# A hybrid decoder trunk on one core: weights in quarters, eight token transfers on two queues, and the first unit copied ahead of the last squares

## The reference, cut to what matters

```python
def rmsnorm(x, g):
    x32 = x.astype(jnp.float32)
    y = x32 * lax.rsqrt(jnp.mean(x32 * x32, axis=-1, keepdims=True) + EPS)
    return (y * g.astype(jnp.float32)).astype(x.dtype)
...
def token_mixers(a, W, i, C0, n0, m0, S0):
    z = a @ W['w_in'][i]
    mq, mk, mv, mi, mf, mo, gq, gk, gv, glr, gg, ga, gb = jnp.split(z, SPLIT_IDX, axis=-1)
...
def trunk(x, p, C0, n0, m0, S0, cv0, W):
    h = x
    for i in range(DEPTH):
        a = rmsnorm(h, W['norm_mix_g'][i])
        mix, C, n, m, Sf = token_mixers(a, W, i, C0[i], n0[i], m0[i], S0[i])
        h = h + mix
        f, cv = conv_ffn(rmsnorm(h, W['norm_ffn_g'][i]), W, i, cv0[i])
        h = h + f
        e = rmsnorm(h, W['norm_ple_g'][i])
        h = h + jax.nn.sigmoid(e @ W['w_ple_gate'][i]) * (p[i] @ W['w_ple_proj'][i])
    y = rmsnorm(h, W['final_norm_g'])
```

## Time and profile before

| | us |
|---|---|
| median of 3 runs | 1178.58 (1177.72 to 1179.01) |
| the profiled execution's own time | 1177.82 |
| its span | 1176.0 |
| PE busy in the span | 1166.6 |
| DVE busy | 756.6 |
| ACT busy | 393.9 |

### The profile page before, as it was taken

How to read it: one execution, slowest core, us unless ns; L and a number is a source line. 1 busy time by engine, 2 the same in 40 slices (tenths; PEclk the granted TensorE clock), 3 DMA queues, 4 the chain that set the end, 5 groups by cost and what they waited for, 6 DMA issues and landing times.

```text
span 1176.0 us, 21858 instructions
## 1 busy us (share of the span) xinstructions
PE 1166.6 (99%) x9191; PEld 1110.7 (94%) x9191; DVE 756.6 (64%) x1394; ACT 393.9 (33%) x579; POOL 4.4 (0%) x9
## 2 busy tenths in 40 slices
PE   9999999999999999999999999999999999999997
PEld 8999999999999999999999999999999999999997
DVE  6855568675777655664665667777777764233677
ACT  6243332133444322333333223333333322111545
POOL 0000000000000000000000000000000000000001
PEclk9999999999999999999999999999999999999999
DMA  6342232422313366554443542122122134223232
GB/s 221 109 150 84 97 108 91 145 73 93 113 68 109 113 223 238 179 171 142 151 143 130 174 155 72 72 76 104 72 75 105 62 102 147 94 75 114 72 108 82
DMA packets 48962, 138.56 MB, mean 118 GB/s; under 512 B 5460, under 2 KB 25108, under 8 KB 39776
## 3 DMA queue, kind: packets, MB, share of 16 engines
q1 hardware_dynamic: 16680, 89.65, 22.0%
q10 hardware_dynamic: 32184, 47.51, 12.0%
HBM read 113.15 MB, written 23.81 MB: 116 GB/s over the span
## 4 chain that ended last, share of the span: by engine, by line
PE 95%; DVE 2%; issue 1%; DMA 1%; ACT 1%; POOL 0%; ACTq 0%; POOLq 0%; DVEq 0%
PE ps L808 34%; PE ps L836 10%; PE ps L834 6%; PE ps L837 6%; PE ps L835 6%; PE ps L937 6%; PE ps L814 6%; PE ps L838 5%; PE ps L943 3%; PE ps L855 2%; PE aux L1100 1%; DMA xT<-in_xT 1%; PE aux L1164 1%; PE aux L995 1%; PE aux L1060 1%
## 5 line engine op out<-in xcount | busy, mean ns | idle before, releaser
L808 PE MATMUL ps<-apair,whi 128*128 128x288 f32 x1728 | 275.1, 298 | 0.7 <-ACT mq L2120 0.6
L808 PEld LDWEIGHTS ps<-apair,whi 128*128 128x128 f32 x1728 | 243.3, 189 | 4.9 <-issue 2.1
L1215 DVE TENSOR_TENSOR wlo<-wraw,whi 128x2048 fp32r<-128x2048 f32 (+1 forms) x82 | 176.1, 2147 | 74.8 <-ACT whi L1965 70.5
L1965 ACT ACTIVATE whi<-wraw 128x2048 fp32r<-128x2048 f32 (+1 forms) x87 | 156.4, 1797 | 107.1 <-PE ps L838 52.5
L836 PE MATMUL ps<-apair,whi 128*128 128x512 f32 x336 | 132.1, 393 | 0.0
L834 PE MATMUL ps<-apair,whi 128*128 128x320 f32 x336 | 105.0, 313 | 0.0
L837 PE MATMUL ps<-apair,wlo 128*128 128x320 f32 x336 | 104.2, 310 | 0.0
L835 PE MATMUL ps<-apair,whi 128*128 128x320 f32 x336 | 103.8, 309 | 0.0
L808 PE MATMUL ps<-apair,wlo 128*128 128x288 f32 x448 | 95.9, 296 | 0.0
L838 PE MATMUL ps<-apair,wlo 128*128 128x256 f32 x336 | 95.1, 283 | 0.0
L838 PEld LDWEIGHTS ps<-apair,wlo 128*128 128x128 f32 x336 | 63.2, 188 | 14.2
(11 more groups left out here) (419 smaller groups left out, 2094.0 us busy)
## 6 DMA issues: line engine op xcount, KB each, us to landing
wraw<-in_w_in SPq DMA_DIRECT2D x31, 1024.0 KB, 5.0
wraw<-in_w_up SPq DMA_DIRECT2D x21, 1024.0 KB, 4.9
gate_scratch<-stg ACTq DMA_DIRECT2D x32, 288.0 KB, 2.8
gt<-gate_scratch ACTq DMA_DIRECT2D x32, 288.0 KB, 2.9
wraw<-in_w_pgate SPq DMA_DIRECT2D x6, 1024.0 KB, 4.7
wraw<-in_w_down SPq DMA_DIRECT2D x8, 704.0 KB, 4.1
wraw<-in_w_down SPq DMA_DIRECT2D x8, 640.0 KB, 3.9
out_C_s<-st ACTq DMA_DIRECT2D x16, 256.0 KB, 3.0
```

Of the source, the lines that this page charges most:

```text
L808: mm = nc.tensor.matmul(ps[:, t % 2, a, 0:HALF], w, x(k)[:, a * HALF:(a + 1) * HALF], start=f, stop=e)
L1215: V.tensor_tensor(wlo[:, s, 0:n], wraw[:, s, 0:n], f32(whi[:, s, 0:n]), ALU.subtract)\
L1965: A.activation(whi[:, s, 0:n], wraw[:, s, 0:n], ACT.Copy).then_inc(split_hi, 1)
```

## The change: what it does

The two halves of unit 0's weights become a quarter, a quarter and a half. The tokens come in eight pieces of one block each. SP issues quarter 0, quarter 1, block 3, the second half, blocks 5 and 7 and the misc weights; ACT issues block 0, the gains, blocks 1 and 2 and, behind its first activation, blocks 4 and 6. DVE, not ACT, copies the high part of quarter 0. PE takes in each block all products of `ahi` before those of `alo`, with a wait for each. ACT copies the two tiles of unit 0 out before the last two squares. `rsum` moves from block 1 to block 3 of unit 1's first tile, `rspread` from block 6 of it to the start of the second tile, and DVE's low part of unit 1 stands ahead of `rsum`.

```diff
-    sched += [("misc",), ("rsum", 0), ("lo", 1), ("rspread", 0), ("misc_scale",)]
+    sched += [("misc",), ("lo", 1), ("rsum", 0), ("rspread", 0), ("misc_scale",)]
...
-MID = {("mq", 1, 0): {1: ("rsum", 0), 6: ("rspread", 0)},
+MID = {("mq", 1, 0): {3: ("rsum", 0)}, ("mq", 1, 1): {0: ("rspread", 0)},
...
-X_PIECES = [(0, 1), (1, 2), (2, 4), (4, 6), (6, 8)]
+X_PIECES = [(k, k + 1) for k in range(KT)]
...
-            sp.dma_start(gains[:, :, :], ins["gains"]).then_inc(gains_in, 16)
...
                 if u == 1:
-                    sp.wait_ge(x_in[3], 16)
+                    sp.wait_ge(x_in[5], 16)
...
                 if u == 0:
-                    sp.dma_start(wraw[:, 0, 0:UW // 2], ins["w_in"][0, :, 0:UW // 2]).then_inc(raw_first, 16)
+                    sp.dma_start(wraw[:, 0, quarter(0)], ins["w_in"][0, :, quarter(0)]).then_inc(raw_first[0], 16)
+                    sp.dma_start(wraw[:, 0, quarter(1)], ins["w_in"][0, :, quarter(1)]).then_inc(raw_first[1], 16)
+                    sp.dma_start(xT[:, 3:4, :], ins["xT"][:, 3:4, :]).then_inc(x_in[3], 16)
                     sp.dma_start(wraw[:, 0, UW // 2:], ins["w_in"][0, :, UW // 2:]).then_inc(raw_in[0], 16)
+                    for k in (5, 7):
+                        sp.dma_start(xT[:, k:k + 1, :], ins["xT"][:, k:k + 1, :]).then_inc(x_in[k], 16)
...
                     if k == 0:
                         pe.wait_ge(hi_first, 1)
+                    elif k == 2:
+                        pe.wait_ge(hi_second, 1)
...
-                    pe.wait_ge(a_hi, k + 1)
-                    pe.wait_ge(a_lo, k + 1)
-                    for n in range(2):
-                        col = (2 * k + n) * P
-                        for x in (ahi, alo):
+                    for x, ready in ((ahi, a_hi), (alo, a_lo)):
+                        pe.wait_ge(ready, k + 1)
+                        for n in range(2):
+                            col = (2 * k + n) * P
...
-                    if k == 0:
-                        pe.wait_ge(lo_first, 1)
+                    if k in (0, 2):
+                        pe.wait_ge(lo_first, k // 2 + 1)
...
                 if s[0] == "norm_in":
+                    dve.wait_ge(raw_first[0], 16)
+                    V.tensor_copy(whi[:, 0, quarter(0)], wraw[:, 0, quarter(0)]).then_inc(hi_first, 1)
                     dve.wait_ge(gains_in, 16)
...
-                        if k == 0:
-                            dve.wait_ge(hi_first, 1)
-                            V.tensor_tensor(wlo[:, 0, 0:UW // 2], wraw[:, 0, 0:UW // 2], f32(whi[:, 0, 0:UW // 2]),
+                        if k < 2:
+                            dve.wait_ge((hi_first, hi_second)[k], 1)
+                            V.tensor_tensor(wlo[:, 0, quarter(k)], wraw[:, 0, quarter(k)], f32(whi[:, 0, quarter(k)]),
...
-            for n, (k0, k1) in enumerate(X_PIECES):
-                act.dma_start(xT[:, k0:k1, :], ins["xT"][:, k0:k1, :]).then_inc(x_in[n], 16)
+            act.dma_start(xT[:, 0:1, :], ins["xT"][:, 0:1, :]).then_inc(x_in[0], 16)
+            act.dma_start(gains[:, :, :], ins["gains"]).then_inc(gains_in, 16)
+            for k in (1, 2):
+                act.dma_start(xT[:, k:k + 1, :], ins["xT"][:, k:k + 1, :]).then_inc(x_in[k], 16)
             act.wait_ge(init_done, 1)
             A.activation(stat[:, 0, :], stat[:, 1, :], ACT.Sqrt).then_inc(act_warm, 1)
+            for k in (4, 6):
+                act.dma_start(xT[:, k:k + 1, :], ins["xT"][:, k:k + 1, :]).then_inc(x_in[k], 16)
...
-                            if k == 0:
-                                act.wait_ge(raw_first, 16)
-                                A.activation(whi[:, 0, 0:UW // 2], wraw[:, 0, 0:UW // 2], ACT.Copy).then_inc(hi_first, 1)
+                            if k == 1:
+                                act.wait_ge(raw_first[1], 16)
+                                A.activation(whi[:, 0, quarter(1)], wraw[:, 0, quarter(1)], ACT.Copy).then_inc(hi_second, 1)
...
                     for k in range(KT):
+                        if k == KT - 2:
+                            for n in range(2):
+                                act.wait_ge(tile_ready, n + 1)
+                                A.activation(two(mq[:, n, :]), tile(n), ACT.Copy).then_inc(tile_free[n], 1)
                         if k >= 2:
                             act.wait_ge(in_sq_used, k - 1)
                         A.activation(sq[:, k % 2, :], xT[:, k, :], ACT.Square).then_inc(in_sq, 1)
```

More of the change, by code:

```diff
@@ L438, in build @@
         raw_in = sems("raw_in", 2)
-        raw_first = sem("raw_first")
+        raw_first = sems("raw_first", 2)
         hi_first = sem("hi_first")
+        hi_second = sem("hi_second")
         lo_first = sem("lo_first")
@@ L591, in both_of, with quarter @@
             return x[:, k - k0, :]
+        def quarter(q):
+            return slice(q * UW // 4, (q + 1) * UW // 4)
         def half_of(e):
@@ L2117, in _ @@
                         act.sem_inc(v_ready, 1)
-                    elif s[1] == 0:
-                        act.wait_ge(tile_ready, tt + 1)
-                        A.activation(two(mq[:, i, :]), tile(tt), ACT.Copy).then_inc(tile_free[tt], 1)
                     elif kind in ("mo", "gg", "ga", "gb"):
```

## The result

| | before | with the change |
|---|---|---|
| median, us | 1178.22 (1177.68 to 1179.01, 22 runs) | 1180.28 (1179.77 to 1181.38, 22 runs) |
| ratio | | 1.0018, 95% interval 1.0012 to 1.0023 |
| the profiled execution, us | 1177.82 | 1179.79 |
| its span, us | 1176.0 | 1178.0 |

I had forecast 1177.7, from a median of 1178.58 of the kernel before that 22 runs put at 1178.22. The time lies above my range, and the change is slower by somewhat more than run-to-run scatter, though by less than 0.2%. The two profiled executions differ by as much as the medians, so the traces can be compared directly. In these two executions the clock plays no part: the page's row reads as before, and the mean granted clock is 0.999 in both.

A forecast was written before the change was run, and what follows sets the result against it. PE was taken as the bound, busy 1166.6 of 1176.0 us. 1.15 (start) + 0.55 (blocks) + 0.55 (`mq`) - 0.5 (`rsum`) - 0.85 (three waits on DVE's chain) = 0.9 us gained: median 1177.7, range 1176.2 to 1179.5.

The forecast's parts named there:

- The bound, and what a gain must pass: Whole kernel: PE is the bound; the opening can give 2.2 us, then PE runs into DVE's chain three times.
- unit 3's low part: DVE's low part ended at 54.99, PE wanted it at 56.58: slack 1.59, gain at most 1.1 us.
- The wait for `mq`: PE before unit 1: the 0.55 us wait goes, since ACT's first copy is done at 21.2, before 21.8.
- First unit, start: PE's first unit starts at 6.75 instead of 7.90 and ends at 19.65 instead of 21.37: 1.7 us gained.
- What follows from the landing: ACT's copy of the second half begins at about 10.2 instead of 11.20, so D = 15.4; no stall on PE.
- The landing itself, 10.2: Second half of unit 0's weights lands at 10.2, taken between estimates of 8.8 and 11.8; before, 9.64.
- D: Time DVE is through with block 7's low part in the opening: forecast 15.4 (bounds 14.4 and 17.0), before 16.42.
- The spread: After `rsum` at 23.95, `rspread` starts at 29.85 and DVE reads it at 30.9; before, 30.37.
- S: How much later DVE's chain runs from its read of the spread on: D - 14.9, not under 0; forecast 0.5 us.
- the wait only changes its place: Rival: D about 16.2, wait at `rsum` and S both 1.3, gain at L1108 0.1, time 1178.5; chance 0.15.
- The slack at the `la` products: Last L1108 pair starts at 70.33, its bank free at 68.96: slack 1.37, gain at most 0.9 us, lasting to the end.
- late-fetch rival: Half lands at 11.8 or later, D 17.0 or more, PE stalls 1 us at block 4, S 2.1, time 1179.3; chance 0.15.

The follow-up runs named there:

- Experiment 8: Kernel before with only the gains moved, from first on SP to behind block 0 on ACT: 1180.39 against 1177.94 us, ratio 1.0017.
- experiment 1: Changed kernel with the load of the gains back at the head of SP's queue: 1180.47 us against 1177.92 for the kernel before, ratio 1.0020.
- 10: Changed kernel without its three token transfers on SP, all eight token blocks on ACT: 1180.19 us against 1178.10 for the kernel before, ratio 1.0019.
- 11: Kernel before with quarters behind the gains on SP, DVE copying quarter 0, reordered passes, one copy ahead, three memsets on GpSimd: 1178.03 against 1177.84 us.
- 9: Kernel before with tokens in eight one-block pieces, all on ACT, and unit 1 released behind block 5: 1177.73 against 1177.84 us, ratio 1.0002.
- 2: Kernel before with the change's order of ACT's copies, `rsum`, `rspread` and unit 1's low part, none of its transfers: 1179.28 against 1177.92 us.
- 4: Changed kernel with three of DVE's opening memsets moved to GpSimd, so DVE's stream is as long as before: 1179.94 us, ratio 1.0016.
- 5: Kernel before with one DVE memset cut into four, three entries more in its stream: 1178.52 against 1178.10 us, ratio 1.0006.
- 3: Changed kernel with the order of before (`sched`, `MID`, copies to `mq`), so the transfers alone: 1179.96 us against 1177.92 for the kernel before, ratio 1.0018.

## Why the prediction was wrong

**The bound, and what a gain must pass: right.** PE is the bound, and the waits of the opening came where the prediction put them, but for one: at `rsum` (forecast 0.5, measured 0.50), at unit 2 and at the `la` products. None was added at unit 3's low part: it came 2.15 late against a slack of 1.59, and PE was already 0.69 late there. The wait for `mq` went (0.55 forecast, 0.63 measured).

**First unit, start: wrong by 1.27 us.** "The gains, now behind block 0 on ACT, are covered in the same way, with about 0.7 us to spare." They land at 7.0, not under 6, and the first product is at 8.02. I took block 0 to land no later than the 4.5 us of the earlier trace rows, although it now stood opposite weights and not the gains; it took 5.2. Experiment 8 shows the place of the gains alone to be enough. It isn't what the 2 us are made of, though: in experiment 1 the start was mended and the time stayed.

**What follows from the landing: the step that failed most.** The landing itself, 10.2, came true. But I let ACT's copy begin at the landing, and dropped what stands ahead of it on ACT: blocks 1 and 2, which I had not given landings of their own. They came at 8.7 and 10.6, the copy at 11.97, and D was 17.18 instead of 15.4. From that copy to D it took 5.2 us, as forecast. What sets D, in the kernels that take the fetch apart:

| | tokens on both queues | tokens on ACT |
|---|---|---|
| gains behind block 0 on ACT | 17.18 (the change) | 17.16 (10), 16.95 (8, halves) |
| gains first on SP | 17.03 (1) | 16.64 (11), 16.20 (9, halves), 16.42 (before) |

Either half of the change's fetch alone holds D at 17. With the gains behind block 0 it is ACT's own queue that is late (in 8 the second half lands at 7.5 and in 10 at 9.1, and its copy begins at 11.4 and 11.9). With the gains first it is the second half (11.8 in 1). Only without both does D come down, with quarters by 0.4 alone, since the half still lands at 11.4 (11), with halves to the 16.4 of before or a little under. No kernel here came near 15.4. What delays the half behind two quarters in 11, where no tokens stand on SP, no run takes apart.

That the landing came true is luck. It was a choice between 8.8 and 11.8, and the 11.8 rests on a wrong reading: the 2.66 MB of before didn't move at 424 GB/s in 6.3 us but at a mean of 276 GB/s in 9.64. The lower bound of 14.4 for D has no working either; a landing at 8.8 would give 14.0.

**The spread: the form was right, the price too small.** My S = D - 14.9 gives 2.3 for D = 17.18, and 2.54 was measured. In all five kernels with the change's order (the change, 1, 2, 4, 10) the scale reaches DVE 15.7 to 15.8 us after D, where my sum has 15.5. I took S to be free until D = 14.9 and believed D to be near it. At the D of the kernel before it is 1.5 by the formula and 1.92 measured: the order loses by itself (0.9 us of waits in experiment 2), and I never worked that case out. The rival "the wait only changes its place" had it at 16.2 and priced it at +0.1 gain.

**The slack at the `la` products: 0.81, not 1.37.** I spaced four pairs that ran side by side by the pitch of products in a row.

**Two stops of DVE: not foreseen.** They cost 0.29 (a step of 0.35, of which 0.06 had come back before it) and 0.36, and moved with the number of entries that DVE has had before (experiments 4 and 5).

The sum: at the `la` products I had 1.37 - 0.5 = 0.87 gained, and it is 0.81 - 2.14 = 1.33 lost, which is 2.2 apart: 1.64 for the delay of DVE's chain (2.14, since the stop at `both`, 0.4, was gone) and 0.56 for the slack. The two stops are 0.65. Together 2.85, and 0.9 forecast gain to 2.0 measured loss is 2.9. The late-fetch rival (D at 17.0 or more, S 2.1, 1179.3) had the mechanism nearly whole. Its place of decision was wrong: it wanted a landing at 11.1, and D came by way of ACT's own queue. Its stall at block 4 didn't come, since PE itself had started 1.27 late. I gave it 0.15.

## What to carry to other kernels

A landing time isn't the time at which work on it starts: list everything that stands ahead on the engine, with a landing for each, and take the latest. Two queues that share the DMA engines are one race: what stands opposite a transfer counts as much as what stands ahead of it, and a tiny transfer that gates the first instruction belongs at the head of a queue, though what stands behind it may then land later (in experiment 1 the second half, at 11.8 instead of 10.2). A step that comes earlier on the bound engine is worth only as much as the next chain can follow, so work out that chain at the old timing too, before believing that a new order is free.

## What the hardware showed that I had not expected

- DVE stops for about half a microsecond, 0.35 to 0.4 of it beyond its usual gap, with nothing to wait for, before records 63, 191, 319 and 1599 of its stream as the trace counts them (one less than a multiple of 64 each, counted from 0), in the kernel before and in all kernels here whose stream is as long as its. In the change, 1, 3, 5 and 10, whose streams are three longer, it stops before 1087 and 1855 (17 and 29 times 64, less one) and not there. All but 191 are 63 more than a multiple of 256. What it waits for, the trace doesn't show, nor why other such places are free of it.
- The same 24 KB landed 2.7 to 2.9 us after issue at the head of SP's queue, and 5.8 to 6.5 us behind one 288 KB block on ACT's.
- Four pairs of 16-row products started within 0.02 us of one another when their banks were free (0.77 us for all eight), and took 1.36 us when they were freed one by one.
- In the profiled execution of experiment 3 PE ran the 32-column misc products, stood idle for 1.14 us, ran four products and 1.1 us of one-column sums, and then had about 3 us at 1.2 GHz (granted clock 1.00 from 24 to 26 us, 0.69 to 28, 0.50 to 30). With the change 1.47 us of idle time before the first unit were followed by no such stretch (granted clock 1.00 from 7 to 14 us). Near the end PE runs 2.3 us of one-column sums: behind them the profiled executions of experiments 2, 8 and 10 have 0.50 from 1170 to 1172 us and that of 9 has 0.50 from 1168 to 1170, where before and the change have 1.00. What decides it, no run here shows.
